# A decoder step: the recurrent stage's gates, decays and scores placed inside the input projection, and two memory projections placed between the heads' steps

## The reference, cut to what matters

```
p_mem_k = einsum('bmd,lde->lbme', mem_prompt, w_mem_k)      # both layers, an output too
p_mem_v = einsum('bmd,lde->lbme', mem_prompt, w_mem_v)

z = rmsnorm(x) @ w_in                                       # 1024 x 3592
q, k, v, o, ig, fg, gb, gc, hb = split(z)                   # 4 heads of 128; ig, fg: 4 columns each
b = cumsum(log_sigmoid(fg)); log_d = b[t] - b[s] + ig[s]    # s <= t
m_t = max(b + m0, max_s log_d)
d = exp(log_d - m_t); inter = exp(b + m0 - m_t)
s = (q k^T) * d                                             # scores
num = s v + inter * (C0 q);  den = sum(s) + inter * (n0 . q)
h = num / max(|den|, exp(-m_t))
C = decay * C0 + (v * w_last)^T k;  n = decay * n0 + w_last k
h = h * rsqrt(mean(h*h)) * head_g;  y_a = sigmoid(o) * h
y_b = gb * conv3(gc * hb)
x = x + [y_a, y_b] @ w_out
```

## Time and profile before

| what | value |
|---|---|
| median of 3 runs | 1567.61 us (1560.7 to 1568.4) |
| profiled execution, its own time | 1564.29 us |
| its span | 1562.4 us |
| mean granted TensorE clock | 0.902 |
| PE busy | 1334.7 us (85%) |
| DVE busy | 591.9 us (38%) |
| ACT busy | 414.7 us (27%) |
| POOL busy | 128.4 us (8%) |

### The profile page before, as it was taken

How to read it: one execution, slowest core, us unless ns; L and a number is a source line. 1 busy time by engine, 2 the same in 40 slices (tenths; PEclk the granted TensorE clock), 3 DMA queues, 4 the chain that set the end, 5 groups by cost and what they waited for, 6 DMA issues and landing times.

```text
span 1562.4 us, 21074 instructions
## 1 busy us (share of the span) xinstructions
PE 1334.7 (85%) x8432; PEld 821.8 (53%) x8432; DVE 591.9 (38%) x1191; ACT 414.7 (27%) x707; POOL 128.4 (8%) x172
## 2 busy tenths in 40 slices
PE   5899996986987959999988977986987959999995
PEld 4787665774665733333335745764665733333333
DVE  2464335544543442222134474423543342122123
ACT  3344331113432301111124312434433211111112
POOL 4001000101000101100101041000000101011000
PEclk9899995557998969999999998977998869999998
DMA  8467540102774506999983646501763605999971
GB/s 244 146 195 239 161 139 28 58 16 70 277 262 150 239 0 275 426 426 427 426 333 113 185 161 220 199 1 31 277 244 147 283 1 231 426 427 426 427 323 35
DMA packets 112224, 339.54 MB, mean 217 GB/s; under 512 B 7406, under 2 KB 75322, under 8 KB 83456
## 3 DMA queue, kind: packets, MB, share of 16 engines
q1 hardware_dynamic: 106560, 320.89, 54.0%
q0 software_dynamic: 5136, 16.26, 3.0%
q10 hardware_dynamic: 432, 1.11, 0.2%
HBM read 327.69 MB, written 10.54 MB: 216 GB/s over the span
## 4 chain that ended last, share of the span: by engine, by line
PE 66%; DMA 15%; DVE 11%; issue 3%; ACT 3%; SPq 1%; POOL 1%; POOLq 0%; DVEq 0%; ACTq 0%
DMA arena<-in_w_exp_up 13%; PE ps L1640 10%; PE ps L518 9%; PE ps L519 9%; PE ps L520 9%; PE ps L1625 2%; PE ps L1689 2%; PE ps L1146 2%; PE ps L1202 2%; PE ps L1121 2%; PE ps L1669 2%; PE ps L1186 1%; PE ps L1107 1%; DMA stg<-in_w_mem_k 1%; PE ps L715 1%
## 5 line engine op out<-in xcount | busy, mean ns | idle before, releaser
L518 PE MATMUL ps<-bx,wh 128*128 128x320 f16 (+1 forms) x832 | 248.9, 299 | 51.9 <-DVE bx L707 27.7
L1640 PE MATMUL ps<-arena,mkv 128*64 128x512 f32 x1024 | 233.1, 608 | 24.0 <-DMA arena<-in_w_exp_up 17.7
L519 PE MATMUL ps<-bx,wh 128*128 128x320 f16 (+1 forms) x832 | 248.8, 299 | 0.0
L520 PE MATMUL ps<-bx,wl 128*128 128x320 f16 (+1 forms) x832 | 248.4, 299 | 0.0
L512 DVE SCALAR_TENSOR_TENSOR wl<-stg,wh 128x1024 f16<-128x1024 f32 x128 | 152.0, 1227 | 147.7 <-ACT wh L505 147.0
L1640 PEld LDWEIGHTS ps<-arena,mkv 128*64 128x64 f32 x1024 | 82.1, 140 | 170.9 <-issue 163.6
L505 ACT ACTIVATE wh<-stg 128x1024 f16<-128x1024 f32 x128 | 128.3, 1049 | 155.1 <-PE ps L520 133.1
L518 PEld LDWEIGHTS ps<-bx,wh 128*128 128x128 f16 x832 | 83.6, 100 | 82.7 <-issue 47.4
L1778 DVE TENSOR_TENSOR arena<-ps,arena 128x512 f16<-128x512 f32 x64 | 44.1, 688 | 143.3 <-ACT arena L1744 92.4
L520 PEld LDWEIGHTS ps<-bx,wl 128*128 128x128 f16 x832 | 83.6, 101 | 27.7
L519 PEld LDWEIGHTS ps<-bx,wh 128*128 128x128 f16 x832 | 83.5, 100 | 27.4 <-issue 0.5
(11 more groups left out here) (379 smaller groups left out, 1769.0 us busy)
## 6 DMA issues: line engine op xcount, KB each, us to landing
arena<-in_w_exp_gate SPq DMA_DIRECT2D x64, 1024.0 KB, 14.8
arena<-in_w_exp_up SPq DMA_DIRECT2D x64, 1024.0 KB, 16.9
arena<-in_w_exp_down SPq DMA_DIRECT2D x32, 1024.0 KB, 17.4
stg<-in_w_exp_down SPq DMA_DIRECT2D x32, 1024.0 KB, 16.7
arena<-in_cache_mem_k SPq DMA_DIRECT2D x16, 1024.0 KB, 7.2
arena<-in_cache_mem_v SPq DMA_DIRECT2D x16, 1024.0 KB, 5.0
stg<-in_w_in_a SPq DMA_DIRECT2D x28, 512.0 KB, 4.8
stg<-in_w_qkv_c SPq DMA_DIRECT2D x20, 512.0 KB, 4.7
```

Of the source, the lines that this page charges most:

```text
L518: nc.tensor.matmul(out, wh[:, s, at:at + 128], hi, start=start, stop=False)
L519: nc.tensor.matmul(out, wh[:, s, at:at + 128], lo, start=False, stop=False)
L520: return nc.tensor.matmul(out, wl[:, s, at:at + 128], hi, start=False, stop=stop)
L1640: last = nc.tensor.matmul(ps[64 * j:64 * j + 64, UB, :], xe[:, q % 2, j, k, :], gu[:, g % 2, j, :, k, :], start=(k == 0), stop=(k == KD - ...
```

## The change

- **Order.** memk1 and memv1 stand behind in_b in the stream. Their eight units (fill) are run one at a time between the heads' steps.
- **Value projections** (memv0, memv1) are computed with tokens on the partitions (value_mm), so that they need no transposes. memk1 is packed two blocks to a bank (packed_mm), and its four transpose groups (keys) stand between heads.
- **First norm.** The input of in_a is x times the norm's gain, split by ACT and DVE into gh and gl; rstd is applied when a unit leaves PSUM, on DVE (unit in mlstm_dve), together with k's scale. The gates are matmuls over xT with the gain folded into wgate. The sum of squares uses four PE matmuls after two additions on POOL.
- **Inside in_a and in_b.** PE runs gates and past after unit 0, columns and token transposes after units 4 to 7, a head's decays after units 5, 6, 7 and in_b's unit 0, scores after in_b's units 0 to 3, the first states after unit 4. DVE and ACT follow the same order. dmat is multiplied in place; qi and qn are made for all heads at once.
- **Heads.** What is left of a head is states, numerators and updates. POOL multiplies the state by its decay and forms the conv input. ACT squares each head as it comes; the state of each head has a place of its own.
- **Tail.** DVE multiplies h by the gate before the norm's root is known; the first unit of out_a takes its conv chunks (4 to 7) first, then chunks 0, 1 and 2, 3 as they are ready.
- SP's wait before the first cache loads has a further condition, the four writes of memory results.

```diff
-STREAM = [("memk0", 4), ("memv0", 4), ("memk1", 4), ("memv1", 4), ("in_a", 8), ("in_b", 6), ("out_a", 4),
+STREAM = [("memk0", 4), ("memv0", 4), ("in_a", 8), ("in_b", 6), ("memk1", 4), ("memv1", 4), ("out_a", 4),
...
+    def packed_mm(s):
+
+        for j in range(2):
+            for k in range(KD):
+                last = mm3(ps[:, s, 256 * j:256 * j + 256], s, k, 128 * j, xh[:, k, 0:256], xl[:, k, 0:256], k == 0,
+                           k == KD - 1)
+        return last
+
+    def value_mm(s, out):
+
+        for t in range(2):
+            r = slice(128 * t, 128 * t + 128)
+            for k in range(KD):
+                c = slice(256 * k, 256 * k + 256)
+                nc.tensor.matmul(out(t), xh[:, k, r], wh[:, s, c], start=(k == 0), stop=False)
+                nc.tensor.matmul(out(t), xh[:, k, r], wl[:, s, c], start=False, stop=False)
+                last = nc.tensor.matmul(out(t), xl[:, k, r], wh[:, s, c], start=False, stop=(k == KD - 1))
         return last
...
+        def decay(h):
+            pool.wait_ge(S["ct_ps"], h + 1)
+            dec = ei[:, h, 320 + NI - 1:384:NI]
+            nc.gpsimd.tensor_tensor(state(h), state(h), dec.unsqueeze(2).to_broadcast([128, NB, 128]), ALU.mult
+                                    ).then_inc(S["decay_ready"], 1)
...
+        def fill(i):
+            u = UK + i
+            pe.wait_ge(S["w_lo"], u * 2 + 2)
+            pe.wait_ge(S["w_ev"], u - 1)
+            if i < 4:
+                last = packed_mm(u % 2)
+            else:
+                last = value_mm(u % 2, lambda t: ps[:, u % 2, 256 * t:256 * t + 256])
+            last.then_inc(S["w_used"], 1)
...
+        for i in range(8):
+            unit(UA + i)
+            if i == 0:
+                gates()
+                past()
+            if i == 4:
+                columns()
+                tokens(0)
+            if i == 5:
+                tokens(1)
+                tokens(2)
+                decays(0)
+            if i == 6:
+                tokens(3)
+                decays(1)
+            if i == 7:
+                tokens(4)
+                tokens(5)
+                decays(2)
+        for i in range(6):
+            unit(UB_ + i)
+            if i == 0:
+                decays(3)
+            if i < 4:
+                scores(i)
+            if i == 4:
+                states(0)
+        numerators(0)
+        updates(0)
+        fill(0)
+        conv_rows()
+        states(1)
+        fill(1)
+        numerators(1)
+        updates(1)
+        fill(2)
+        states(2)
+        fill(3)
+        numerators(2)
+        updates(2)
+        fill(4)
+        keys(0)
+        states(3)
+        fill(5)
+        keys(1)
+        numerators(3)
+        updates(3)
+        keys(2)
+        fill(6)
...
+        keys(3)
+        fill(7)
+
+        u = UNIT["out_a"][0]
+        pe.wait_ge(S["w_lo"], u * 2 + 2)
+        pe.wait_ge(S["w_ev"], u)
+        for n, ks in enumerate(((4, 5, 6, 7), (0, 1), (2, 3))):
+            pe.wait_ge(S["in_lo"], IN["out_a"][0] + n + 1)
+            last = unit_mm(0, T, ah, al, ks=ks, k0=4, k1=3)
+        last.then_inc(S["w_used"], 1)
+        pe.wait_ge(S["n_ready"], 1)
+        pe.wait_ge(S["tr_ev"], G_MK1 + 4)
+        gemm_pe(pe, "out_a", src=(ah, al), first=1)
...
+        V = nc.vector
+        r = rstd[:, 1, :].unsqueeze(1).to_broadcast([128, 2, T])
+
+        def unit(u):
+            dve.wait_ge(S["w_used"], u + 1)
+            if u == UA:
+                split_lo(dve, u + 2, u % 2)
+                dve.wait_ge(S["std_ready"], 2)
+            c = 2 * (u - UA)
+            k = 128 ** -0.5 if 4 <= c < 8 else 1.0
+            b = 2 * (u % 2)
+            V.scalar_tensor_tensor(z[:, c:c + 2, :], ps[:, b:b + 2, 0:T], k / WSCALE, r, ALU.mult, ALU.mult
+                                   ).then_inc(S["w_ev"], 1)
+            if u != UA:
+                split_lo(dve, u + 2, u % 2)
+
+        def fill(i):
+            split_lo(dve, UK + i + 2, (UK + i) % 2)
...
+        for i in range(2, 5):
+            unit(UA + i)
+        dve.wait_ge(S["ml_ps"], 2)
+        V.tensor_copy(acol[:, 0:8], ps[:, 7, 0:8])
+        V.tensor_copy(acol[0:64, 8:12], ps[0:64, 7, 8:12]).then_inc(S["ml_ev"], 1)
+        tokens(0)
+        unit(UA + 5)
+        tokens(1)
+        tokens(2)
+        unit(UA + 6)
+        tokens(3)
+        unit(UA + 7)
+        tokens(4)
+        tokens(5)
+        dve.wait_ge(S["out_mem"], 32)
+        unit(UB_)
+        unit(UB_ + 1)
+        dve.wait_ge(S["ei_ready"], HA)
+        V.tensor_copy(wlast[0:64, :, 0:8], dmat[0:64, :, 384 + NI - 1:448:NI])
+        V.tensor_copy(wlast[:, :, 8:10], dmat[:, :, 255:384:128])
+        link(V.tensor_tensor(qi[:], zq[:, :, NP:T], ei[:, :, 320:384], ALU.mult))
+        n0v = n0T.rearrange("p (b h) -> p h b", h=HA)
+        for h in range(HA):
+            last = V.tensor_tensor(qn[:, h].rearrange("p (b i) -> p b i", b=NB),
+                                   qi[:, h].rearrange("p (b i) -> p b i", b=NB),
+                                   n0v[:, h].unsqueeze(2).to_broadcast([128, NB, NI]), ALU.mult)
+        last.then_inc(S["q_ready"], 1)
+        dve.wait_ge(S["q_ready"], 1)
+        scores(0)
+        unit(UB_ + 2)
+        scores(1)
+        unit(UB_ + 3)
+        scores(2)
+        dve.wait_ge(S["osig_ready"], 1)
+        link(V.tensor_scalar(zo[:], zo[:], 0.5, 0.5, ALU.mult, ALU.add))
+        unit(UB_ + 4)
+        scores(3)
+        dve.wait_ge(S["w_used"], UB_ + 6)
+        weighted(0)
+        unit(UB_ + 5)
+        outputs(0)
+        updates(0)
+        weighted(1)
+        gated(0)
+        fill(0)
+        dve.wait_ge(S["ml_ps"], 3)
+        V.tensor_copy(cout, ps[0:48, 3, :]).then_inc(S["ml_ev"], 1)
+        conv(0)
+        fill(1)
+        outputs(1)
+        updates(1)
+        weighted(2)
+        gated(1)
+        fill(2)
+        conv(1)
+        fill(3)
+        outputs(2)
+        updates(2)
+        weighted(3)
+        gated(2)
+        fill(4)
+        for n in range(2):
+            dve.wait_ge(c_out[n], 16)
+        keys(0)
+        conv(2)
+        fill(5)
+        keys(1)
+        outputs(3)
+        updates(3)
+        gated(3)
+        conv(3)
+        keys(2)
+        dve.wait_ge(S["in_hi"], IN["out_a"][0] + 1)
+        V.tensor_sub(al[:, 4:8], xn[:, 4:8], ah[:, 4:8]).then_inc(S["in_lo"], 1)
+        fill(6)
         dve.wait_ge(S["ml_ps"], 4)
-        nc.vector.tensor_copy(nout[0:36, :], ps[0:36, 3, 0:128]).then_inc(S["n_ready"], 1)
-
-        dve.wait_ge(S["osig_ready"], 1)
-        link(nc.vector.tensor_scalar(zo[:], zo[:], 0.5, 0.5, ALU.mult, ALU.add))
+        V.tensor_copy(nout[0:36, :], ps[0:36, 2, 0:128]).then_inc(S["n_ready"], 1)
+        keys(3)
+        fill(7)
         dve.wait_ge(S["hstd_ready"], 1)
-        link(nc.vector.tensor_tensor(xn[:, 0:4, :], xn[:, 0:4, :], hstd, ALU.mult))
-        for h in range(HA):
-            v = VEC["head"] + h
-            last = nc.vector.scalar_tensor_tensor(xn[:, h, :], xn[:, h, :], vec[:, v:v + 1], zo[:, h, :], ALU.mult,
-                                                  ALU.mult)
-        last.then_inc(S["y_ready"], 1)
+        V.tensor_tensor(xn[:, 0:4, :], zo[:], hstd, ALU.mult).then_inc(S["y_ready"], 1)
         dve.wait_ge(S["y_ready"], 1)
-
+        for n, k in enumerate((slice(0, 2), slice(2, 4))):
+            dve.wait_ge(S["in_hi"], IN["out_a"][0] + n + 2)
+            V.tensor_sub(al[:, k], xn[:, k], ah[:, k]).then_inc(S["in_lo"], 1)
```

More of the change, by code:

```diff
@@ L111 @@
 _at = 0
-for _n, _w in (("in_a", 2), ("out_a", 2), ("memq0", 4), ("memo0", 2), ("qkv", 4), ("out_c", 2), ("memq1", 4),
+for _n, _w in (("in_a", 4), ("out_a", 3), ("memq0", 4), ("memo0", 2), ("qkv", 4), ("out_c", 2), ("memq1", 4),
                ("memo1", 2)):
@@ new lines, in mlstm_pool @@
+        pool.wait_ge(S["ei_ready"], HA)
+        decay(0)
+        pool.wait_ge(S["w_ev"], sum(UNIT["in_b"]))
+        pool.wait_ge(S["ml_ev"], 1)
+        nc.gpsimd.tensor_tensor(u_p[:, :, 2:], zgc[:, :, 0:NP], zhb[:, :, 0:NP], ALU.mult)
+        for c in range(4):
+            last = nc.gpsimd.tensor_tensor(u_s[:, c, :, 2:], zgc[:, c, NP:T].rearrange("p (b i) -> p b i", b=NB),
+                                           zhb[:, c, NP:T].rearrange("p (b i) -> p b i", b=NB), ALU.mult)
+        link(last)
@@ L913, in mlstm_pe, with conv_rows @@
             for i in range(2):
-                last = nc.tensor.matmul(ps[:, 3, 136:137], kt[:, i, :], dmat[:, h, 255 + 128 * i:256 + 128 * i],
-                                        start=(i == 0), stop=(i == 1))
+                last = nc.tensor.matmul(ps[:, 2, 136:137], kt[:, i, :], wlast[:, h, 8 + i:9 + i], start=(i == 0),
+                                        stop=(i == 1))
             last.then_inc(S["cn_ps"], 1)
+        def conv_rows():
+            pe.wait_ge(S["u_ready"], 1)
+            for c in range(4):
+                last = nc.tensor.transpose(ps[0:48, 3, 128 * c:128 * c + 128], cv[:, c, :], ident)
+            last.then_inc(S["ml_ps"], 1)
```

(34 more changed lines are left out.)

567 lines of the change are left out of this document (310 added, 257 removed).

## The result

| | before | after |
|---|---|---|
| median | 1568.01 us (1560.7 to 1571.48, 4 runs) | 1496.01 us (1490.53 to 1500.92, 4 runs) |
| profiled execution, its own time | 1564.29 us | 1494.2 us |
| its span | 1562.4 us | 1492.3 us |
| mean granted clock | 0.902 | 0.926 |
| PE busy | 1334.7 us (85%) | 1296.9 us (87%) |

The change made the kernel faster: ratio 0.9546, interval 0.9497 to 0.9595. The forecast was 1500 us, between 1477 and 1528.

What follows compares the result with a forecast made beforehand. PE in its slow forms (half clock, waits for DVE and ACT) bounds the stage. 88.4 us gained, less 3 for unseen waits, 16 for the heads' clock and 5 for early clock losses, makes 64 us less: 1500 us, range 1477 to 1528.

Steps and rivals of the forecast that it cites:

- What bounds: From the input projections to out_a: PE limits the stage, through half clock in the heads and waits for DVE and ACT.
- The front: Up to in_a: both kernels stand at 81.1 us, the norm's sum takes 2.15 us, late rstd would stall only the second unit.
- PE's list: From 81.1 us to memq0: PE's work at full clock sums to 222 us, so memq0 would start at 303.1 without waits.
- half clock halves: Small PE steps seen at half clock were entered at half their time, giving 11.6 us a head.
- Waits: From in_a to out_a: 4.7 us left uncovered in the tail, plus 3 us for unseen waits (0 to 10).
- The clock: Heads and early small steps: clock losses of 16 us for four heads (0 to 38) plus 5 us elsewhere.
- The gates and early terms: Gates, four decays and the tail's pause: 5 us of clock loss, bounds 0 and 26.
- The clock holds: Rival for the heads: full clock is kept through them, giving 1479 us; chance 0.14.
- the heads stay slow: Rival: heads stay at 1.2 GHz and each first fill starts slow, 1522 us, or 1543 with early terms; chance 0.16.
- DVE paces the heads: Rival: DVE, standing still 13 us beside POOL, limits the heads; some 10 us more, 1510; chance 0.07.
- Each insertion costs the clock: Rival: small PE work runs at half clock and its 19 places each cost 2.05 us, 1579 us; chance 0.02.
- The change doesn't do what it says: Rival: waits on DVE's order lengthen memory units, 3 us for each of 22 units and fills, 1566 us; chance 0.02.

Runs made afterwards that it cites:

- e2: The changed kernel with its eight memory units run in one block ahead of head 0 instead of between the heads' steps; 1529.41 us.
- e1: The kernel before, with 200 useless f16 matmuls added while PE waits for the rows, ahead of the heads and in each head; 1547.14 us.
- e5: The changed kernel run again without any change, as partner of three further kernels on its chip; 1496.23 us.
- e8: The changed kernel with the states' decay multiplied on DVE instead of POOL; 1499.09 us.
- e6: The changed kernel with a memory unit between each head's numerators and updates, and the next unit halved around the next states; 1490.87 us.
- e7: The changed kernel with the last memory unit moved ahead of the heads' sums, no longer beside the norm's root; 1498.66 us.
- e3: The changed kernel with token transposes, decays, scores and first states moved out of in_a and in_b to one run behind them; 1525.63 us.

## Why the prediction was right, step by step

It gave memq0's first matmul near 332 us; it came at 322.7. The 9 us between them come out of the terms as follows.

- **What bounds.** PE in its two slow forms, half clock and waits. e2 brings both back by moving eight units alone, and e1 gains from the clock alone. Shown.
- **The front.** in_a began at 84.9 us, not 83.3; memv0's last unit had ended late, at 82.75. In e5 it began at 81.0, so this is scatter. rstd never held a unit up. The gates took 4.5 us at 1.00, 4.4 forecast.
- **PE's list: 222 us forecast, some 227 measured.** Taking 11.0 us of clock loss and 3.7 of idle time from the 241.6 us between 81.1 and 322.7 leaves 226.9. Of the 4.9 us more, 1.6 are the late start. The rest is the rule "half clock halves": at 1.00 a head's numerators took 4.5 us and not 8.46 / 2 = 4.23, its updates 3.4 and not 3.16, its decays 2.59 and not 4.54 / 2 = 2.27. That makes 0.8 a head, 3.3 in all. These small matmuls took a little more than half of their time when the clock doubled.
- **Waits: 4.7 + 3 forecast, 3.7 measured.** The tail's was nearly right: 0.7 ahead of the first half unit and 3.0 behind it. Its sum has a slip: its pieces add to 13.1 us and not 13.6, and 13.6 less the cover of 9.1 is 4.5 and not 4.7. The trace has 12.8 us from the end of the sums (284.3) to the first matmul on the new input (297.1); the splits took 3.9 us of it, not 5. The 3 us for waits that I could not see were not there: the only other gap, 1.0 us, is the handover to memq0, which the list has. That is 4.0 less.
- **The clock: 21 us forecast, 11.0 in this profile, 20.7 in the second one** (heads 97.3 - 90.7 + 9.3 = 15.8, units behind decays 1.7 + 1.5, the tail 1.7). The 4 us a head were the middle of a wide range, and the measured price is not spread so: a head either keeps the clock, at no cost, or loses it near the end of its numerators (head 2 of e5 at the start of its updates), for 4.65 to 6.3 us (head 1 of e5, with a fill of 8.0 us behind it). The gates and early terms (5) came to 1.7 and 4.9. In the first profile this term is 10 us less than forecast.
- **Sum:** 81.1 + 222 + 7.7 + 21 = 331.8 was forecast, and 331.8 + 4.9 - 4.0 - 10.0 = 322.7. That the list's 4.9 and the waits' 4.0 nearly cancel is luck, and so is that 20.7 in the second profile lies next to the 21: two executions of one program differ by 10 us in this term.
- **The rest of the kernel**, taken as unchanged, took 1169.6 us after memq0's start against 1166.2. In the other profiles it took between 1166.5 (e8) and 1170.5 (e1, which has before's order), so the 3.4 us are no effect of the change. They turn 73.5 us into 70.1 in the span and 1494.2 in the execution's own time, 6 us under the 1500; the median is 4 under. The term that was mis-sized is the clock's.

The rivals. *The clock holds* (1479) and *the heads stay slow* (1522) were both right of some heads: with two of four losing it, after lies between. e2 shows what the second would have looked like for the heads as a block (0.53). *DVE paces the heads*: DVE was busy 66.65 of 90.2 us (64 of 84 forecast), and in neither profile of after did PE wait for it before the tail. The lock with POOL exists, and cost DVE 44 x (1353 - 1221) ns = 5.8 us in all, not 13, none of it on PE's path. *Each insertion costs the clock* (1579): the decays cost it twice of four times in e5 and never in the first profile; the fall needed 12 of 19 places and had at most six. *The change doesn't do what it says*: a fill took 5.4 us between first matmul and last at 1.00.

I said that the heads' stage would take 95 to 105 us; it took 90.7 and 97.3. The mean clock of 0.75 to 0.9 held: 0.89 and 0.82.

The Trainium skill, "TensorE: Matmul & The Clock Gate", section "Why this matters for your kernels", has a rule that PE keeps its full clock while there are no idle gaps in it. The traces disagree: after's head 1 ran without any gap (11.20 of 11.20 us busy) and fell to 0.50 inside it. Only the other half of the rule, that a gap costs the clock, agrees with a row here: e1's fall at 341.4 us, after PE had stood idle since 337.0.

What stays open is why one head loses the clock and its neighbour, with the same instructions and the same fill before it, doesn't. Where in a head it falls is known better. In the profiles of after, e5, e6, e7, e8 and, from head 1 on, e3, it fell in 15 of 23 heads, each time between 3.3 and 5.1 us after the head's first numerator: behind the sixteen matmuls of 8 columns, which fill the time from 1.1 to 2.9 us. The number of heads differs from execution to execution (2, 3, 1, 2, 4 of four, and 3 of three). Nor was it tried which of the small matmuls in a head (those of 8 columns, the float32 ones, the transposes) counts least.

## What to carry to other kernels

When a stage is slow because its engine waits and its clock is down, put dense independent matmul work between its small steps, not before or behind them: here the same eight units made the kernel 33 us faster between the heads than as a block ahead of them. Price a clock loss as an event (here some 5 us a head: half the small work after the fall and the slow start of what follows), not as a rate, and leave the range wide enough for one execution to have three such events and the next one six. Two repairs of the same loss don't add: undo them alone and together before a gain is put down to either.

## What the runs showed of the hardware

- Useless f16 matmuls made a kernel faster: 200 of them, 16.8 us less (e1).
- DVE and POOL stood still for each other, in both directions. Two places in after, DVE's line of time (start, us) and POOL's:

```profile
202.45 2.34 DVE L517 SCALAR_TENSOR_TENSOR wl<-stg,wh 128x1024 f16<-128x1024 f32 x2
...
214.87 3.91 DVE L517 SCALAR_TENSOR_TENSOR wl<-stg,wh 128x1024 f16<-128x1024 f32 x2 [2.78 <-ACT wh L510]
```

```profile
202.61 4.40 POOL L859 TENSOR_TENSOR arena<-arena 128x1024 f32<-128x1024 f32 x1 [6.92 <-DVE arena L1173]
...
214.66 1.91 POOL L852 TENSOR_TENSOR arena<-arena 128x1024 f32<-128x1024 f32 x1 [2.75 <-PE ps L962]
```

At 202 us DVE was first: its pair of splits kept its 2.34 us and POOL's conv product took 4.40. At 214 us POOL was first: its decay took 1.91 us, and DVE's pair 3.91. In both the one that began second waited. The Trainium skill, "SBUF — State Buffer", section "Who interferes with whom", says just that of a DVE instruction with two SBUF inputs and a POOL instruction that reads SBUF; these rows agree with it.
- The wait can outlast one instruction. In e3 DVE's L1184 (64 x 1024, both inputs in SBUF; 1.21 us in the other heads) took 6.31 us, from 220.21 to 226.52 us, beside a run of POOL's instructions that had begun at 218.63 and went on through the decay (1.92 us), the conv product (2.34 us, where it took 4.40 in after) and four short ones. DVE stood still for some 5.1 us, although the decay and the product began after it; the first two of the run, which began before it, are issues of DMAs.

- POOL's multiply of 1024 columns took 1.91 us, below the 2.6 that I had scaled from 1.64 us for 640.
